# A hybrid DeltaNet and ConvGLU layer on one core: order of the last loads of the scan, place of one weight split, and 64 waits ahead of TensorE's program

## The chip, the cores and the metric

One core of a Trainium2 chip runs the whole layer in one launch. The metric is the device time of the launch in microseconds.

## What is computed

One layer (DEPTH = 1) of a trunk, for 1024 latent tokens (rows of 64) and 128 context tokens that share the weights:

```python
def mixer(h, row_len, s0_f, s0_b, w_in, conv_a_w, qkv_conv_w, a_log, dt_bias, o_norm_w, w_out):
    z = h @ w_in
    ...
    y_conv = cb * row_conv3(cc * cx, conv_a_w, row_len)
    qkv = jax.nn.silu(row_conv3(qkv, qkv_conv_w, row_len)).astype(jnp.float32)
    ...
    o_f, s_f = chunked_gated_delta(q, k, v, beta[:, :, 0], log_alpha[:, :, 0], s0_f)
    ...
    o = rmsnorm(o, o_norm_w) * jax.nn.silu(gate.astype(jnp.float32).reshape(b, l, DN_HEADS, DV))
    y = jnp.concatenate([y_conv, o.reshape(b, l, V_W).astype(h.dtype)], axis=-1) @ w_out
    return y, s_f, s_b

def conv_glu(h, row_len, w_up, ffn_conv_w, w_down):
    u, gt = jnp.split(h @ w_up, 2, axis=-1)
    gt = grid_conv3x3(gt, ffn_conv_w, row_len)
    return (jax.nn.gelu(gt) * u) @ w_down
```

The width is 1024, there are 4 heads of 128, the FFN width is 2816. Around the mixer and the ConvGLU stand RMS norms with shift, scale and gate from `silu(c) @ w_ada + b_ada`. The delta rule runs forward and backward in chunks of 64. Outputs are the two streams after a last norm and the scan's final states of the context tokens.

## The kernel before, in words

Everything is kept with channels on partitions and the 1152 tokens on the free axis, in 3 thirds of 384 or in 9 tiles of 128 (`TT_` = 9, `LAST` = 8, `HALF` = 4, `EARLY` = 6). Each product is made in three passes of fp32r matmuls, with the weights and the activations split in a high and a low part. A *unit* is a 128 x 1024 piece of weights: SP loads it into `raw`, ACT copies the high part (`high`, L1478 to L1481), POOL subtracts to get the low part (`low`, L1280 to L1283), and TensorE waits for the latter (`wl_ready`) and multiplies in `product_step` (L2360 to L2370; L2368 is the matmul with the high activations, L2370 the one with the low ones). Units 0 to 28 are the input projection, `U_OUT` = 29 to 36 the output projection, the rest the FFN. Ahead of all this TensorE makes the modulation rows (`ada_unit`, L2302 to L2309): the weights for them come through a ring of four buffers, whose next load waits until a unit is used.

The order of the work is written out by hand for each engine. Between the input and the output projection lies the scan, with a function for each engine: `delta_pe` (L1147), `delta_act` (L838), `delta_dve` (L925), `delta_pool` (L696), and the loop at L613 on SP. Each runs over x = -1 to 8; with y = x + 1, a round does the serial step x for both directions d = 0, 1 and prepares what step y needs. Direction 0 takes tile y, direction 1 tile 7 - y, and both take tile 8 (the context) last. The steps that matter here, with `seen(eng, what, d, n)` as the wait for the n-th of a kind:

- SP, for each y: the decay rows of both directions into `gb` (L618, waits for `q_decayed` of the round before), `LZ` (L623), keys and values `kv` (L629), queries `q` (L636; direction 0 also waits for `trq`, the turned queries of the round before). At y = 1 the first two gate tiles `og` follow (`og_load`, L608 to L611). At y = 7 and y = 8 half each of the convolution output `ycA` follows (L645, 1152 KB each). Behind the loop come the gate tiles of index 1, 2, 3 and the last, then `ycB`, three units and `X` for the residual.
- POOL: the mask on the decay rows (`masked`, L688), later scale and square of finished tiles (L707, L702), and the decayed queries (`decayed`, L694, waits for `gb_exp` of ACT). At x = 2 the low half of unit 30 (`U_OUT + 1`) stands at the end of the round.
- ACT: exponentials of the masked rows (`exps`, L816), the new values (L874), off-diagonal blocks (L748, L752), `gb_exps` (L824), key scaling (`key_end`, L863), copies (L870, L844), squares of the turned queries (L834), the corner copy (L761), then logarithm and root for the norm (L850, L855). At x = 1 the high half of unit 30 stands behind the key scaling.
- DVE: from x = 6 on, `finish` (L968) multiplies a turned tile with the gate tile `og`; further `diagonal` (L987), `low_diagonal` (L998), `values` (L1007), `weights` (L1021), `second_out` (L953), sums of squares (L960, L962) and the state (L942, L945).
- TensorE: matmuls of the scan (`by_head`, L1157), transposes (`turn`, L1152), the 32-wide products (L1102, L1116, L1118), third and fourth products (L1130, L1142, L1144). `queries` at y = 8 waits for `o_final`, which `finish` gives.

Behind the scan come the output projection (the first pair begins with k = 0 on `ycA` and waits for the state), the second norm, and the FFN in a hardware loop of five turns on each engine (`pe.Fori(0, GROUPS)`, L2618): on TensorE 8 blocks of 72 matmuls and 8 of 36 in each turn, which does 4 of the FFN's 22 column blocks.

```python
            def og_load(d, t, i):
                if i and i < 3:
                    seen(sp, "o_final", d, i)
                sp.dma_start(gate_tile(d, i)[:], g_d[:, :, t * P:t * P + P]).then_inc(s[gate_landed(d, i)], 16)
```

## Time and profile before

| | us |
|---|---|
| median of 3 runs | 1610.46 (1606.65 to 1616.3) |
| the profiled execution | 1610.77 |
| its span, first to last instruction | 1608.8 |
| TensorE matmuls busy | 1533.7 |
| DVE / ACT / POOL busy | 938.6 / 484.4 / 409.1 |
| granted TensorE clock, mean | 0.981 |

Times in the trace are microseconds from the start of the span. PE is TensorE's matmul side and PEld its weight loads, SPq is the queue side of SyncE (the time in which it issues a DMA), "issue" is time in which an engine waited for nothing that the profile shows. A number in brackets behind a row is the idle time of the engine just before it, with what ended it. The granted clock is 1.00 at 2.4 GHz and 0.50 at 1.2 GHz. By time the span falls into the modulation rows and the first norm (0 to 50), input projection (50 to 483), scan (483 to 624), output projection and second norm (624 to 760), FFN (760 to 1570) and the last products and norm.

### The profile page before, as it was taken

The numbers are of one execution on the slowest core, as the hardware profiler recorded it, in microseconds if no ns is written. First come the engines' busy times: TensorE is split into PE (matmuls) and PEld (weight loads), VectorE is DVE, ScalarE is ACT, GpSimd is POOL, SyncE is SP. The second block draws the span as 40 slices with busy tenths as digits, with TensorE's granted clock in tenths as the row PEclk, the third lists the DMA queues.
The fourth block names the chain that finished last, engine by engine and source line by source line (L and its number), as shares of the span: only waits on it lengthen the run. The fifth ranks groups of instructions, "written<-read, shape, count | busy, mean of one in ns | idle before, by whom it ended". The sixth has DMA issues, their size and how long they took to land.

```text
span 1608.8 us, 24001 instructions
## 1 busy us (share of the span) xinstructions
PE 1533.7 (95%) x9744; PEld 1475.7 (92%) x9744; DVE 938.6 (58%) x1398; ACT 484.4 (30%) x904; POOL 409.1 (25%) x204
## 2 busy tenths in 40 slices
PE   5899999999999988999999999999999999999997
PEld 1798999999989877998999999999999999999996
DVE  2752453669997874337875276536643673467257
ACT  4331254221257674225221212121212210222024
POOL 0011111650223552230232132113221421222220
PEclk9899999999999998999999999999999999999999
DMA  9544224542434556110111111111111111111103
GB/s 350 191 184 153 89 73 132 161 125 72 140 118 132 158 185 261 40 66 1 53 40 40 51 37 45 40 41 40 40 40 41 40 53 40 41 40 40 40 1 118
DMA packets 74640, 142.87 MB, mean 89 GB/s; under 512 B 19228, under 2 KB 44900, under 8 KB 72868
## 3 DMA queue, kind: packets, MB, share of 16 engines
q1 hardware_dynamic: 70932, 134.00, 24.7%
q10 hardware_dynamic: 3168, 5.51, 0.9%
q8 instruction: 86, 1.41, 0.4%
q0 software_dynamic: 432, 1.77, 0.3%
q14 instruction: 22, 0.18, 0.0%
HBM read 120.60 MB, written 20.65 MB: 88 GB/s over the span
## 4 chain that ended last, share of the span: by engine, by line
PE 81%; DVE 8%; DMA 4%; ACT 3%; issue 2%; POOL 1%; SPq 1%; DVEq 0%; ACTq 0%; POOLq 0%
PE ps L2368 49%; PE ps L2370 24%; DMA araw<-wts 2%; PE ps L1157 2%; PE ps L2309 1%; DVE ptmp L1978 1%; DVE lanes L1982 1%; PE ps L2319 1%; DMA og<-gd 1%; PE ps L2576 1%; DVE fa L2203 1%; POOL qd L694 1%; PE ps L2477 0%; PE ps L2436 0%; DMA q<-q_d 0%
## 5 line engine op out<-in xcount | busy, mean ns | idle before, releaser
L2368 PE MATMUL ps<-hH,wH 128*128 128x384 f32 x1680 | 570.0, 339 | 8.0 <-DVE hL L1807 3.6
L2370 PE MATMUL ps<-hL,wH 128*128 128x384 f32 x1680 | 565.8, 337 | 7.2 <-issue 7.2
L1283 POOL TENSOR_TENSOR wL<-raw,wH 128x1024 fp32r<-128x1024 f32 x93 | 225.9, 2429 | 906.5 <-ACT wH L1481 906.0
L2368 PE MATMUL ps<-hH,wL 128*128 128x384 f32 x1680 | 384.4, 336 | 0.0
L2368 PEld LDWEIGHTS ps<-hH,wH 128*128 128x128 f32 x1680 | 318.4, 190 | 15.8 <-issue 13.3
L1481 ACT ACTIVATE wH<-raw 128x1024 fp32r<-128x1024 f32 x99 | 105.1, 1061 | 739.8 <-PE ps L2368 738.7
L2370 PEld LDWEIGHTS ps<-hL,wH 128*128 128x128 f32 x1680 | 318.6, 190 | 8.5 <-issue 8.5
L2203 DVE SCALAR_TENSOR_TENSOR fa<-G,cst,fa 128x1024 f32<-128x1024 f32 x176 | 302.2, 1717 | 15.4 <-DVE fa L2200 0.6
L2368 PEld LDWEIGHTS ps<-hH,wL 128*128 128x128 f32 x1680 | 302.1, 189 | 0.0
L2368 PE MATMUL ps<-pH,wH 128*128 128x384 f32 x528 | 179.2, 339 | 4.1 <-DVE pL L2227 1.9
L2090 DVE SCALAR_TENSOR_TENSOR X<-ps,mod,X 128x384 f32<-128x384 f32 x138 | 70.5, 567 | 187.2 <-PE ps L2368 187.2
L2370 PE MATMUL ps<-pL,wH 128*128 128x384 f32 x528 | 177.1, 335 | 0.0
L2368 PE MATMUL ps<-pH,wL 128*128 128x384 f32 x528 | 123.0, 335 | 0.0
L2199 DVE TENSOR_SCALAR fa<-G,cst 128x1024 f32<-128x1024 f32 x22 | 16.6, 753 | 172.2 <-ACT G L1497 172.2
L2368 PEld LDWEIGHTS ps<-pH,wH 128*128 128x128 f32 x528 | 99.6, 189 | 7.0 <-DVE X L2092 3.2
L2370 PEld LDWEIGHTS ps<-pL,wH 128*128 128x128 f32 x528 | 99.5, 189 | 0.7
L2368 PEld LDWEIGHTS ps<-pH,wL 128*128 128x128 f32 x528 | 94.8, 189 | 0.0
L1839 DVE TENSOR_SCALAR acc<-zp,wqk 128x1024 f32<-128x1024 f32 (+1 forms) x24 | 21.8, 946 | 72.8 <-ACT zp L1497 72.8
L1342 POOL TENSOR_TENSOR pL<-fa,pH 128x1152 fp32r<-128x1152 f32 x16 | 58.9, 3680 | 12.3 <-ACT pH L1701 12.3
L2309 PE MATMUL ps<-araw,scT 128*32 128x512 f32 x192 | 37.3, 675 | 18.2 <-DMA araw<-wts 18.2
L2220 DVE TENSOR_TENSOR fa<-fa,ps 128x384 f32<-128x384 f32 x66 | 32.6, 550 | 20.0 <-PE ps L2368 20.0
L2309 PEld LDWEIGHTS ps<-araw,scT 128*32 128x32 f32 x192 | 5.9, 114 | 41.3 <-DMA araw<-wts 29.1
(326 smaller groups left out, 1872.7 us busy)
## 6 DMA issues: line engine op xcount, KB each, us to landing
raw<-wts SPq DMA_DIRECT2D x103, 512.0 KB, 3.3
araw<-wts SPq DMA_DIRECT2D x48, 512.0 KB, 6.2
X<-xT SPq DMA_DIRECT2D x8, 1152.0 KB, 14.5
kv<-tok_d SPq DMA_DIRECT2D x16, 512.0 KB, 5.1
tok_d<-stage ACTq DMA_DIRECT2D x18, 256.0 KB, 2.1
q<-q_d SPq DMA_DIRECT2D x18, 256.0 KB, 6.8
gb<-grow_d SPq DMA_DIRECT2D x18, 256.0 KB, 3.8
y<-X SPq DMA_DIRECT2D x8, 384.0 KB, 2.4
```

What stands on the lines that cost most here:

```text
L1157: last = M(ps[:, k, h * P:h * P + P], left(h), right(h), start=(start if start is not None else h == 0), stop=(stop if stop is not None el ...
L1283: nc.gpsimd.tensor_tensor(weight(1, u4), raw[:, u4 % RAW, :], weight(0, u4).bitcast(F32), ALU.subtract).then_inc(s["wl_ready"], 1)
L1342: nc.gpsimd.tensor_tensor(pL[:, slot, :], fa[:, f % 2, :], pH[:, slot, :].bitcast(F32), ALU.subtract).then_inc(s["pL_ready"], 1)
L1481: A(weight(0, u4), raw[:, u4 % RAW, :], ACT.Copy).then_inc(s["wh_ready"], 1)
L1839: last = V.tensor_scalar(dst, src, w(tap), None, ALU.mult)
L2090: last = V.scalar_tensor_tensor(xs(lo, hi), bank3(side, n)[:, 0:hi - lo], mod[:, gate * 8 + ob, 0:1], xs(lo, hi), ALU.mult, ALU.add)
L2199: V.tensor_scalar(dst, src, w(3 * dy + dx), None, ALU.mult)
L2203: last = V.scalar_tensor_tensor(dst, src, w(3 * dy + dx), dst, ALU.mult, ALU.add)
L2220: last = V.tensor_tensor(fa[:, f4 % 2, n * TW:n * TW + TW], fa[:, f4 % 2, n * TW:n * TW + TW], bank3(side, n), ALU.mult)
L2309: last = M(ps[o:o + Q, ada_bank(m), :], scT[:, kt, :], araw[:, a % ARAW, 512 * j:512 * j + 512], start=(kt < 2), stop=(kt >= KT - 2))
L2368: last = M(out, lhs, rh[:, c], start=(k == 0 and not lo), stop=(lo and k == kts - 1))
L2370: M(out, lhs, rl[:, c], start=False, stop=False)
```

## The change

- On SP, y = 8 begins with the two gate tiles of index 1, which stood behind the loop, and the query load of direction 0. The query load of direction 1 for y = 8 is left out (its only readers are at y < 8).
- The two loads of `ycA` go from SP to ACT, at the beginning of its rounds x = 5 and x = 7, with the same waits.
- On POOL, the low half of unit 30 goes from the end of round x = 2 to right behind the masks of that round. On ACT, its high half goes from behind the key scaling of round x = 1 to behind the corner copy.
- TensorE's program begins with 128 waits for `bias_set`, which DVE sets with its third instruction; two waits go into one instruction, so that there are 64 instructions more.

```diff
+N_PAD = 128
@@ SP
+            def q_load(d, y):
+
+                t = tile_of(d, y)
+                seen(sp, "qk", d, min(y, HALF))
+                seen(sp, "q_decayed", d, y)
+                if d == 0:
+                    sp.wait_ge(s["trq"], y)
+                sp.dma_start(dl[d]["q"][:], q_d[:, :, t * P:t * P + P]).then_inc(s[f"q_in_{d}"], 16)
+
             for y in range(1, TT_):
+                if y == LAST:
+                    for d in range(2):
+                        og_load(d, tile_of(d, 5), 1)
+                    q_load(0, y)
                 for d in range(2):
...
-                for d in range(2):
-                    b, t = dl[d], tile_of(d, y)
-                    seen(sp, "qk", d, min(y, HALF))
-                    seen(sp, "q_decayed", d, y)
-                    if d == 0:
-                        sp.wait_ge(s["trq"], y)
-                    sp.dma_start(b["q"][:], q_d[:, :, t * P:t * P + P]).then_inc(s[f"q_in_{d}"], 16)
+                if y < LAST:
+                    for d in range(2):
+                        q_load(d, y)
...
-                if y in (HALF + 3, HALF + 4):
-                    k = y - HALF - 3
-                    seen(sp, "pt", 1, (HALF + 2, LAST)[k])
-                    sp.dma_start(ycA[:, 2 * k:2 * k + 2, :].bitcast(F32), yc_d[:, 4 * k:4 * k + 2, :].bitcast(F32)).then_inc(s["ycA_in"], 16)
-            for d in range(2):
-                og_load(d, tile_of(d, 5), 1)
@@ POOL
+                if x == 2:
+                    low(U_OUT + 1, U_OUT + 1)
                 for d, t, i in summed(x - 1):
                     scale(d, t, i)
...
-                if x == 2:
-                    low(U_OUT + 1, U_OUT + 1)
@@ ACT
+                if x in (HALF + 1, LAST - 1):
+                    k = (HALF + 1, LAST - 1).index(x)
+                    seen(act, "pt", 1, (HALF + 2, LAST)[k])
+                    act.dma_start(ycA[:, 2 * k:2 * k + 2, :].bitcast(F32),
+                                  yc_d[:, 4 * k:4 * k + 2, :].bitcast(F32)).then_inc(s["ycA_in"], 16)
                 if 0 < y < TT_:
                     exps(y)
...
-                    if y == 2:
-                        high(U_OUT + 1, U_OUT + 1, 0)
...
                     corner(y)
+                if y == 2:
+                    high(U_OUT + 1, U_OUT + 1, 0)
@@ TensorE
+            for _ in range(N_PAD):
+                pe.wait_ge(s["bias_set"], 1)
             pe.wait_ge(s["sc_ready"], 2)
             for a in range(KT + 1):
                 ada_unit(a)
```

## Rows read from the trace of the kernel before

**Rows 1.** The page, busy time by engine.
```profile
PE 1533.7 (95%) x9744; PEld 1475.7 (92%) x9744; DVE 938.6 (58%) x1398; ACT 484.4 (30%) x904; POOL 409.1 (25%) x204
```
**Rows 2.** Waits of TensorE, 480 to 625: us in total, times, longest.
```profile
PE ps L2368 <- DVE S L942: 7.0, 1, 7.0
PE ps L1157 <- DVE oTok L968: 6.6, 1, 6.6
PE ps L1157 <- ACT Y L874: 3.4, 2, 2.8
```
**Rows 3.** Chain of waits, 583 to 604: start us, us, what.
```profile
584.53 2.95 POOL qd L694
...
591.77 0.61 SPq L645
...
592.43 9.72 DMA og<-gd
```
**Rows 4.** Timeline of DVE, ACT and TensorE, 579 to 611: start us, us, instructions.
```profile
579.79 1.41 DVE L968 SCALAR_TENSOR_TENSOR oTok<-ps,onw,og 128x512 f32<-128x512 f32 x2
...
591.81 2.44 ACT L816 ACTIVATE R<-R,SC 128x128 f32<-128x128 f32 x8
...
596.68 0.27 ACT L752 ACTIVATE TX<-ps 32x128 f32<-32x128 f32 x1
...
602.24 1.57 DVE L968 SCALAR_TENSOR_TENSOR oTok<-ps,onw,og 128x512 f32<-128x512 f32 x2 [6.92 <-DMA og<-gd]
...
608.99 1.06 PE L1152 MATMUL ps<-cst,q 128*128 128x128 f32 x4
...
610.08 0.28 ACT L834 ACTIVATE ptmp<-ps 128x128 f32<-128x128 f32 x1 [10.67 <-PE ps L1152]
```
**Rows 5.** Windows: busy time of each engine, granted clock, DMA share, GB/s.
```profile
603.00:606.00 3.00, 2.75 (x15) 2.56 (x16) 1.95 (x3) 0.00 (x0) 0.00 (x0) 0.50 0.45 122
```
**Rows 6.** Timeline of ACT, TensorE, POOL and DVE around unit 30, 504 to 524.
```profile
504.02 1.04 ACT L1481 ACTIVATE wH<-raw 128x1024 fp32r<-128x1024 f32 x1
...
505.83 0.63 PE L1152 MATMUL ps<-cst,q 128*128 128x128 f32 x4 [0.66 <-ACT KQ L870]
...
520.94 2.36 POOL L1283 TENSOR_TENSOR wL<-raw,wH 128x1024 fp32r<-128x1024 f32 x1
...
521.42 2.74 DVE L987 TENSOR_TENSOR raw<-XT,cst 128x512 f32<-128x512 f32 x1
```
**Rows 7.** Waits of TensorE in the FFN loop, 760 to 1400.
```profile
PE ps L2370 <- issue: 7.2, 4, 2.2
PE ps L2368 <- issue: 2.5, 4, 0.9
```
**Rows 8.** Timeline of TensorE at the second turn of the FFN loop.
```profile
1073.16 0.43 PE L2368 MATMUL ps<-hH,wH 128*128 128x384 f32 x1 [0.91 <-issue]
...
1076.24 0.69 PE L2370 MATMUL ps<-hL,wH 128*128 128x384 f32 x1 [1.94 <-issue]
```
**Rows 9.** Windows of 6 us behind the first three turns.
```profile
921.00:927.00 6.00, 6.00 (x26) 6.00 (x27) 2.73 (x4) 2.78 (x6) 1.56 (x1) 0.72 0.28 90
1076.00:1082.00 6.00, 5.75 (x18) 5.76 (x19) 3.13 (x4) 2.38 (x6) 1.15 (x1) 0.50 0.25 90
1232.00:1238.00 6.00, 5.52 (x24) 5.52 (x25) 2.76 (x4) 2.76 (x6) 1.52 (x1) 0.72 0.27 90
```
**Rows 10.** DMA view 1070 to 1078 (queue: packets, MB, share); windows between instruction packets.
```profile
q8 instruction: 3, 0.05, 2.2%
...
1007.00:1029.00 22.00, 21.68 (x125) 21.36 (x125) 13.90 (x19) 3.29 (x3) 4.80 (x2) 1.00 0.15 49
1051.40:1070.60 19.20, 19.20 (x113) 19.20 (x112) 3.59 (x8) 1.06 (x1) 2.38 (x1) 1.00 0.18 55
```
**Rows 11.** TensorE's first matmul, and a wait by itself in SP's chain of waits.
```profile
5.42 1.92 PE L2309 MATMUL ps<-araw,scT 128*32 128x512 f32 x4 [5.42 <-DMA araw<-wts]
...
589.32 0.02 SPq L386
589.34 0.03 issue
```

## The prediction

> **What bounds the kernel now.** I read the views in this order: the page, the waits of TensorE by stage, the chain of waits, the timeline of the delta stage, the granted clock by window, and the DMA view of the instruction queue. The page says that TensorE is busy for 95% of the span [rows 1], so a gain has to come from one of its few idle stretches or from a stretch at the lower clock. The waits of the delta stage (480 to 625) name two of about 7 us: one before L2368, which is the end of the scan, and one before L1157, put down to DVE's L968 [rows 2]. The chain shows what L968 itself waited for: POOL's second product of round y = 7 ends at 587.49, SP then works through its list for y = 8, reaches the convolution load at 591.77 and the gate loads at 592.43, and the gate tile lands 9.72 us later, at 602.15 [rows 3]. Round y = 8 therefore stands still: DVE is idle for 6.92 us, from 595.3 to 602.24 [rows 4]. The wait before L2368 is a chain of small steps on ACT, POOL and DVE and is not touched. The third place is the FFN loop: at each of its four turns TensorE stops twice with no releaser, 2.5 us in all for the first stops and 7.2 us for the second ones [rows 7].
>
> **The gate loads, the query load and the convolution output on ACT's queue.** SP now issues the two gate loads as the first thing of y = 8. They need the first two tiles finished (L968, at 579.8 to 581.2 [rows 4]), so they go out at about 581.5, while SP has nothing to send until 584.6, and land by about 591 even if they take the 9.72 us of the old ones. Nothing is queued behind them that was ready earlier. Next, the query load of direction 0 waits for the turned queries of y = 7, which PE finishes about 585.4; the decay row of direction 0 behind it then leaves at about 586.1 instead of 584.6, and its mask at 589.4. That is not late, for ACT starts the exponentials only at 591.81 [rows 4]. The decay row of direction 1 waits for the POOL product that ends at 587.49 as before. The query load of direction 1 is dropped; nobody waits for it.
> The convolution load moves to ACT, ahead of the exponentials of y = 6 and y = 8. At y = 6 ACT waits for a mask there anyway, so I cost it at nothing; without that cover it costs the 0.61 us that SP needs for it [rows 3]. At y = 8 it is on the path: 0.61 us. What comes out: DVE runs L968 at 595.35 and 596.1 instead of 602.24; off-diagonal blocks on ACT end at 597.6 instead of 596.95 [rows 4], and now the third products wait for them. Then come third products (0.6 at the full clock), the copy (0.4), second third products and copy (to 599.5), two weights of 0.65 (to 600.8), and the turned queries at 600.8 instead of 608.99 [rows 4]: 8.2 us earlier. The part after the old wait ran at the lower clock, 0.50 [rows 5], which the shorter idle time avoids, and this is why the shift exceeds the wait. From L834 (610.08) on, everything is the old chain, shifted. I take **7.5 us**, bounds 6.0 (the wait less the ACT issue) and 8.5. What is late next is the off-diagonal block on ACT.
>
> **Unit 30.** ACT's high half (0.95 to 1.04 us) stands today between the key scaling and the copy for which TensorE waits 0.66 us at 505.83 [rows 6]. Moved behind the corner copy it falls into 1.5 us in which ACT waits for PE: gain **0.7 us**, bounds 0 and 1.0. POOL's low half (2.36 us at 520.94) moves some 11 us ahead, into idle time before the products of y = 3, which wait for ACT until 518.2: cost nothing; if that cover were gone, 2.4 us. Today it lies beside DVE's L987, which takes 2.74 us instead of about 1.05 [rows 6]. By the Trainium skill (SBUF — State Buffer, on the shared port pair) a GpSimd instruction and a DVE instruction with two SBUF inputs shut each other out; the row agrees. But TensorE has no gap there, and ACT takes up the result only 0.3 us after it was free, so I book no gain for it. A stall of 2.8 us at 548.6 [rows 2] starts with the POOL products of y = 4 that take 5.95 us beside DVE's work. A shift of under 1 us may or may not dissolve it; I leave it, and keep 2.8 us for the range.
>
> **64 instructions at TensorE's head.** 128 waits for a semaphore set at 0.9, two in one instruction. TensorE starts at 5.42, released by a DMA [rows 11], so 4.4 us of cover. A wait that stands by itself on SP takes 0.05 us (0.02 and an issue of 0.03) [rows 11]: 64 of them 3.2 us. Cost nothing; uncovered, all of what exceeds 4.4 us, since the loads behind the first unit wait for it.
> What they do is move the rest of TensorE's program by 64 places. The instruction queue brings 0.05 MB in 3 packets, 16 to 17 KB each, around the turn at 1073 [rows 10]. In steady running a packet comes each 22 us, in which the window counts 125 matmuls and as many weight loads [rows 10], so a packet holds about 250 instructions. At the turn one packet goes out at 1070.6, TensorE restarts at 1073.16, runs 5 matmuls and stops 1.94 us [rows 8]; the next packet is at 1074.0 and it runs on 2.2 us later. So the border between two packets lies 5 matmuls behind the head of the loop, and the second one is asked for only when the first is entered. With 64 instructions in front, that border moves 32 matmuls back, ahead of the loop's head, and the next is about 95 matmuls (16 us) behind the head, which hides a fetch of 2.2 us. The four second stops go: **7.2 us** [rows 7]. With them goes the slow clock behind them: 6 us at 0.72, 0.50 and 0.72 after the first three turns are 1.7, 3.0 and 1.7, together **6.4 us** [rows 9]; the fourth had 1.00.
> What may come back is at the first stop. Before the turn the last border is 19.2 us (113 matmuls) back [rows 10]; the 64 instructions add 32 matmuls to that, which is more than one packet holds, so one more border comes to stand 7 to 15 matmuls (1.2 to 2.6 us) before the turn. A fetch takes 2.2 to 2.6 us from packet to use, so the fetch for what follows the loop may be under way when the turn asks for its own. Bounds 0 and 1.4 us each turn; no row shows two fetches at once, I take the middle, **2.8 us** back for four. Net 10.8, bounds 13.6 and (if the gap stays and takes the clock with it) about 0.
>
> **The sum.** The profiled execution took 1610.77 us (span 1608.8, 2.0 around it), 0.3 above the median of 1610.46. 1610.8 - 7.5 - 0.7 - 10.8 = 1591.8, taken as 1592.
>
> **The rivals.** *A: the loop gives nothing.* The second stop belongs to the turn and not to the border, or the first one grows by as much. For it: I know the borders only from packet times. Against it: the stop came after exactly 5 matmuls each time, and the packet stands in it. 1610.8 - 8.2 = 1602.6. The Trainium skill (Runtime: NRT & Kernel Launch, "Instruction fetch mechanics") has fetches in blocks of 256 instructions, calls a crossing mostly hidden and makes only the taken branch outside the window dear; by its words alone this rival holds, while the size of block agrees with the packets. Chance 0.18.
> *B: another load takes the place of the gate tile.* Keys and values for y = 8 leave SP at 590 and the convolution output still goes at 591.8, onto the same 16 engines; if values landed at 600, the tail would give 3 and the total 1596. Against it: two query tiles and two gate tiles less are on the engines then. Chance 0.12.
> *C: slower.* The waits at the head are dear. They decide from 0.07 us each on, and make the whole slower than before from (19.0 + 4.4) / 64 = 0.37 us each. At the 0.61 us of an instruction that SP issues [rows 3] they take 39 us, 34.6 beyond the cover: 1592 + 34.6 = 1627. Against it: the 0.05 us of SP's wait. Chance 0.03.
> *D: the stall of y = 4 goes too*, 1589. Chance 0.10. The forecast has 0.57.
>
> **How the numbers follow.** The forecast's own bounds are 1610.8 - 8.5 - 0.7 - 13.6 = 1588 and 1610.8 - 6.0 - 8.0 = 1597. B lies inside; D at the good end reaches 1585, and A lies at 1602.6 (at worst 6.0 alone, 1604.8), so the range goes from 1585 to 1603.5; C is left out. A measurement of this kernel can tell 0.5%, 8 us, from no change. Forecast, B and D are faster than 1602.4; A lies on that bound and is split, a third of it faster. Faster 0.85, same 0.12, slower 0.03.
>
> **What would show it.** Right: no wait of DVE L968 for the gate load of 7 us; L1152 near 600; a single stop per turn in the loop, under 2 us, followed by a clock of 1.00; first matmul still at 5.4; the two POOL masks of y = 4 no later than 523.3. Wrong: two stops per turn, or one of 3 us with the clock at 0.5 behind it; L1157 before the last round waiting for ACT or a DMA for over 3 us; the first matmul after 6 us.

## The result, and the profile after

| | before | changed |
|---|---|---|
| median, us | 1610.75 (1606.65 to 1616.3, 4 runs) | 1593.2 (1591.28 to 1595.0, 4 runs) |
| ratio | | 0.9889, interval 0.9856 to 0.9921 |
| profiled execution, us | 1610.77 | 1592.61 |
| span, us | 1608.8 | 1590.7 |
| TensorE matmuls busy, us | 1533.7 | 1524.4 |
| granted clock, mean | 0.981 | 0.985 |

The change makes the kernel 17.5 us faster, 1.1%; the forecast was 1592.0. That the sum is right does not say that its terms are: the loop gave more than its term and the scan less, as the section on the prediction shows. The page, busy time by engine, against [rows 1]:

```profile
PE 1524.4 (96%) x9744; PEld 1471.3 (92%) x9744; DVE 936.8 (59%) x1398; ACT 484.4 (30%) x904; POOL 403.1 (25%) x204
```

The same number of matmuls takes 9.3 us less, so about half of the gain is work done at a higher clock, the rest idle time that has gone.

**By stage.** Each cut is an instruction that is easy to find in the timelines: the first matmul of the first norm's output (hH), ACT's first exponentials (those of y = 1), its exponentials of y = 7 and of y = 8, the first matmul on `ycA`, and the first matmul on `pH`, the input of the FFN's second product. The last cut lies some 90 us behind the start of the loop, within its first turn, so the first FFN products belong to the row of the output projection. Below, "FFN" is the stretch from that cut to the end; all four returns to the head of the loop lie in it. The first stretch counts from the start of the span.

| us | before | changed | difference |
|---|---|---|---|
| start to the first matmul on hH | 50.6 | 47.2 | -3.4 |
| to the exponentials of y = 1 | 426.8 | 427.6 | +0.8 |
| rounds: exponentials of y = 1 to y = 7 | 98.8* | 100.2 | +1.4 |
| last stretch: y = 7 to the first matmul on ycA | 48.0 | 42.5 | -5.5 |
| output projection, second norm, first FFN products | 230.2 | 232.9 | +2.7 |
| rest of the FFN and the end | 754.3 | 740.3 | -14.0 |

(* the six rounds took 15.0, 16.8, 16.0, 16.5, 15.8 and 18.7 before; 16.1, 16.9, 15.0, 16.5, 16.8 and 18.9 after.)

**The FFN loop.** Waits of TensorE, 760 to 1400, in the changed kernel (engine, line, waited for: us in total, times, longest). Against [rows 7] the line of the second stops, 7.2 us in four, is gone; the first ones, 2.5 us before, are as they were:

```profile
PE ps L2379 <- issue: 2.3, 4, 0.8
```

The timeline of TensorE at the first turn, changed kernel (start us, us, instructions, idle before). One stop, and then it runs on; before, there was a second one after the fifth matmul [rows 8]:

```profile
913.99 0.43 PE L2379 MATMUL ps<-hH,wH 128*128 128x384 f32 x1 [0.44 <-issue]
914.26 0.34 PE L2381 MATMUL ps<-hL,wH 128*128 128x384 f32 x1
914.44 0.35 PE L2379 MATMUL ps<-hH,wH 128*128 128x384 f32 x1
914.62 0.34 PE L2381 MATMUL ps<-hL,wH 128*128 128x384 f32 x1
914.80 0.34 PE L2379 MATMUL ps<-hH,wH 128*128 128x384 f32 x1
914.98 0.33 PE L2381 MATMUL ps<-hL,wH 128*128 128x384 f32 x1
```

The windows of 6 us behind the first three turns, changed kernel (us, busy time and count of PE, PEld, DVE, ACT and POOL, granted clock, DMA share, GB/s). They had a clock of 0.72, 0.50 and 0.72 with 26, 18 and 24 matmuls [rows 9]:

```profile
914.80:920.80 6.00, 6.00 (x36) 6.00 (x36) 0.93 (x2) 4.86 (x8) 2.40 (x1) 1.00 0.18 61
1066.00:1072.00 6.00, 6.00 (x37) 6.00 (x36) 0.95 (x2) 4.75 (x8) 2.40 (x1) 1.00 0.21 57
1217.00:1223.00 6.00, 6.00 (x36) 6.00 (x36) 0.94 (x2) 4.86 (x8) 2.39 (x1) 1.00 0.20 61
```

**The end of the scan.** Timeline of SP, POOL, ACT, DVE and TensorE, 579 to 602, changed kernel. The gate tiles go out at 579.11 and DVE's `finish` (now L977) waits for the turned tile, 0.31 us, and no longer for the load, 6.92 us [rows 4]. The turned queries come at 601.02 and ACT's squares at 601.72, against 608.99 and 610.08 [rows 4]:

```profile
579.11 1.76 SPq L612 DMA_DIRECT2D og<-gd  x2
...
589.33 1.27 POOL L692 TENSOR_TENSOR R<-gb,cst 128x512 f32<-128x512 f32 x1 [5.48 <-DMA gb<-grow_d]
...
590.97 1.28 ACT L859 ACT_TABLE_LOAD   x1
...
590.99 0.33 ACTq L885 DMA_DIRECT2D ycA<-yc  x1
...
595.66 1.41 DVE L977 SCALAR_TENSOR_TENSOR oTok<-ps,onw,og 128x512 f32<-128x512 f32 x2 [0.31 <-PE ps L1161]
...
601.02 0.66 PE L1161 MATMUL ps<-cst,q 128*128 128x128 f32 x4 [0.62 <-DVE PT L1030]
...
601.72 0.28 ACT L838 ACTIVATE ptmp<-ps 128x128 f32<-128x128 f32 x1 [1.81 <-PE ps L1161]
```

Waits of TensorE, 480 to 625, changed kernel. Of the three in [rows 2] the middle one is gone; the one at the end of the scan and the one of y = 4 (2.8 us, for the new values of ACT) stand:

```profile
PE ps L2379 <- DVE S L951: 7.0, 1, 7.0
PE ps L1166 <- ACT Y L878: 2.9, 2, 2.8
```

**The head.** Waits of TensorE, 0 to 60, changed kernel, and its first matmul, which stood at 5.42 [rows 11]. It now starts at 8.01, released by nothing that the profile shows: TensorE's sequencer was still going through the 64 instructions. The third view below lists 63 instructions that do nothing but wait (the last of the 128 waits share instructions with what follows): 51 ns each, the first starting at 1.0 and the last at 7.7, so one in 0.11 us.

```profile
PE ps L2318 <- DMA araw<-wts: 11.0, 6, 5.2
PE ps L2318 <- issue: 8.0, 1, 8.0
```

```profile
8.01 1.93 PE L2318 MATMUL ps<-araw,scT 128*32 128x512 f32 x8 [8.01 <-issue]
```

```profile
L2333 PEldq EVENT_SEMAPHORE  x63: 51/51/51, 1.0 to 7.7; - x63
```

### The profile page after: what moved, and what is told of

It is laid out like the page before. It is cut to its first block, busy times and chain, and to the rows that moved or that the text cites. A ratio compares the mean times of both kernels' runs of the same rounds, so it can differ in the third digit from the quotient of the medians.

```text
span 1590.7 us, 24063 instructions
## 1 busy us (share of the span) xinstructions
PE 1524.4 (96%) x9744; PEld 1471.3 (92%) x9744; DVE 936.8 (59%) x1398; ACT 484.4 (30%) x904; POOL 403.1 (25%) x204
## 4 chain that ended last, share of the span: by engine, by line
PE 85%; DVE 7%; ACT 2%; issue 2%; DMA 2%; POOL 1%; DVEq 0%; ACTq 0%; SPq 0%; POOLq 0%
PE ps L2379 50%; PE ps L2381 25%; PE ps L1166 4%; DMA araw<-wts 2%; PE ps L2318 1%; DVE ptmp L1987 1%; DVE lanes L1991 1%; PE ps L2328 1%; POOL qd L698 1%; PE ps L2587 1%; DVE fa L2212 1%; DMA gb<-grow_d 1%; PE ps L2488 1%; PE ps L2447 0%; DVE XT L1998 0%
## 5 line engine op out<-in xcount | busy, mean ns | idle before, releaser
L2212 DVE SCALAR_TENSOR_TENSOR fa<-G,cst,fa 128x1024 f32<-128x1024 f32 x176 | 295.9, 1681 | 15.4 <-DVE fa L2209 0.6
L1351 POOL TENSOR_TENSOR pL<-fa,pH 128x1152 fp32r<-128x1152 f32 x16 | 55.5, 3471 | 21.1 <-ACT pH L1710 21.1
L2318 PE MATMUL ps<-araw,scT 128*32 128x512 f32 x192 | 33.5, 664 | 19.1 <-DMA araw<-wts 11.0
```

Of the source, the lines that this page charges most:

```text
L1351: nc.gpsimd.tensor_tensor(pL[:, slot, :], fa[:, f % 2, :], pH[:, slot, :].bitcast(F32), ALU.subtract).then_inc(s["pL_ready"], 1)
L2212: last = V.scalar_tensor_tensor(dst, src, w(3 * dy + dx), dst, ALU.mult, ALU.add)
L2318: last = M(ps[o:o + Q, ada_bank(m), :], scT[:, kt, :], araw[:, a % ARAW, 512 * j:512 * j + 512], start=(kt < 2), stop=(kt >= KT - 2))
```

## The experiments

Twelve kernels in three sets. The kernel before ran beside each set: 1610.05 (1601.82 to 1617.7, 29 runs) for the first four, 1608.63 (1603.27 to 1610.42, 11) for the next four, 1611.27 (1601.7 to 1617.23, 11) for the last. One kernel's executions spread by up to 0.6% to either side, so a difference of 2 or 3 us between two medians tells little alone; below, the stages of the profiles are read beside it. The three sets ran on different chips. A comparison across sets is safer by what each kernel gains on the kernel before of its own set, and where the text gives such a gain it is the difference of the two medians. The ratios in the table differ slightly from the ratios of these medians; by its ratio the kernel with the waits alone gains 9.7 us and not 11.3.

| kernel | median us (lowest to highest, runs) | ratio to before, interval |
|---|---|---|
| waits only | 1598.8 (1592.58 to 1608.49, 12) | 0.994, 0.9917 to 0.9963 |
| all but the waits | 1604.72 (1597.34 to 1608.14, 12) | 0.9967, 0.9946 to 0.9989 |
| waits later | 1593.25 (1591.8 to 1594.7, 4) | 0.9897, 0.9857 to 0.9937 |
| 4 instructions, not 64 | 1609.0 (1600.2 to 1611.66, 10) | 0.9985, 0.9962 to 1.0009 |
| gate and query loads early | 1587.21 (1586.02 to 1590.46, 4) | 0.987, 0.9849 to 0.989 |
| unit 30 moved | 1596.46 (1594.09 to 1599.09, 6) | 0.9928, 0.991 to 0.9946 |
| convolution output on ACT | 1600.52 (1593.84 to 1606.86, 6) | 0.9943, 0.9922 to 0.9964 |
| decay rows before the query | 1593.06 (1590.76 to 1599.12, 6) | 0.9916, 0.9896 to 0.9937 |
| convolution output back on SP | 1590.39 (1585.78 to 1598.31, 6) | 0.9871, 0.9839 to 0.9903 |
| only its second half on ACT | 1594.58 (1590.33 to 1598.13, 6) | 0.9893, 0.9864 to 0.9923 |
| last diagonal block later | 1589.34 (1587.4 to 1591.96, 6) | 0.9863, 0.9835 to 0.9891 |
| the change once more | 1593.11 (1589.74 to 1595.76, 6) | 0.9883, 0.9854 to 0.9912 |

The stages of their profiles in us, cut as above. "3-4" is from the exponentials of y = 3 to those of y = 4; "last" is y = 7 to the first matmul on `ycA`, with the part behind the exponentials of y = 8 in brackets.

| kernel | start to hH | to y = 1 | 3-4 | last (behind y = 8) | output, to pH | FFN, from pH |
|---|---|---|---|---|---|---|
| before | 50.6 | 426.8 | 16.0 | 48.0 (32.5) | 230.2 | 754.3 |
| changed | 47.2 | 427.6 | 15.0 | 42.5 (25.0) | 232.9 | 740.3 |
| waits only | 53.5 | 428.2 | 16.0 | 43.7 (25.9) | 230.0 | 740.6 |
| all but the waits | 52.9 | 427.0 | 15.0 | 40.1 (24.0) | 232.9 | 750.4 |
| waits later | 52.9 | 426.3 | 15.0 | 41.8 (23.5) | 230.4 | 740.7 |
| 4 instructions | 48.1 | 427.7 | 15.0 | 41.0 (23.9) | 230.4 | 758.8 |
| gate and query early | 48.7 | 426.8 | 16.0 | 39.3 (24.0) | 232.7 | 740.2 |
| unit 30 moved | 51.7 | 426.6 | 15.0 | 49.0 (33.4) | 230.0 | 740.9 |
| conv. on ACT | 53.3 | 428.1 | 16.0 | 48.4 (32.7) | 232.9 | 740.5 |
| rows before query | 49.6 | 427.6 | 15.0 | 42.5 (27.2) | 232.8 | 740.4 |
| conv. back on SP | 52.5 | 428.4 | 15.0 | 40.1 (25.0) | 234.1 | 741.2 |
| second half on ACT | 49.4 | 426.3 | 15.0 | 41.9 (26.8) | 230.0 | 740.6 |
| diagonal later | 48.6 | 428.9 | 15.0 | 41.6 (26.0) | 229.9 | 740.6 |
| change once more | 49.1 | 428.4 | 15.0 | 40.1 (25.0) | 232.7 | 740.0 |

### First set: the waits

**The waits alone**, in the kernel before.

```diff
+N_PAD = 128
...
+            for _ in range(N_PAD):
+                pe.wait_ge(s["bias_set"], 1)
             pe.wait_ge(s["sc_ready"], 2)
```

> The kernel before with the 128 waits alone. Border theory (the waits move the border between two instruction packets away from the loop's head): in the FFN loop one stop per turn instead of two, no slow clock behind the turns, and from the first product with pH to the end 14 us less than before; the scan as before. Head theory (the later start of the modulation rows, 8.0 instead of 5.4 us, lets the loads of X through): the first product with hH at about 47 instead of 50.6. Both together 1595; if the waits only move the border and the head is chance, 1597. Rival (the loop's gain needs the other edits): 1608 or more.

Measured: 1598.8, that is 11.3 us below 1610.05. The FFN takes 740.6 instead of 754.3. The first matmul on hH was expected at about 47 by the theory that the later start lets other loads through; it came at 53.5, so that theory is out. Waits of TensorE in the loop: one kind of stop is left.

```profile
PE ps L2371 <- issue: 2.7, 4, 0.9
```

**Everything but the waits.**

```diff
-            for _ in range(N_PAD):
-                pe.wait_ge(s["bias_set"], 1)
             pe.wait_ge(s["sc_ready"], 2)
```

> The changed kernel without the waits at the head. Border theory: two stops per turn as before, 2.5 and 7.2 us; the scan shorter by some 2 to 7 us. If the recorded sum were right (the tail of the scan gives 7.5 and unit 30 gives 0.7) the time is 1602.5; if the profile of the changed kernel is typical (the scan took 1.9 us less in it, and 2.7 were lost behind it) it is 1607 to 1609.

Measured: 1604.72, 5.3 us below the kernel before. Both stops of the loop are there, the second one again behind five matmuls, in the waits and in the timeline of TensorE:

```profile
PE ps L2379 <- issue: 7.5, 4, 2.1
PE ps L2377 <- issue: 2.4, 4, 0.7
```

```profile
913.81 0.44 PE L2377 MATMUL ps<-hH,wH 128*128 128x384 f32 x1 [0.69 <-issue]
...
916.87 0.69 PE L2379 MATMUL ps<-hL,wH 128*128 128x384 f32 x1 [1.92 <-issue]
```

So the two halves of the change each work without the other, and the whole of the loop's gain hangs on the 64 instructions. The FFN takes 750.4 us here and 754.3 before, with the same stops (9.9 and 9.7 us in all): what differs is the clock behind them, as the kernel with 4 instructions shows below. In this profile the round from y = 5 to y = 6 took 13.9 us instead of 15.5 to 17.6 elsewhere, and the next one 20.4 instead of 18.0 to 18.9: what one round wins there, the next gives back.

**The waits later**: not at the start of TensorE's program but behind the second turn of the modulation rows, so that the first matmul is not held up and the rest of the program is moved by the same 64 places.

```diff
-            for _ in range(N_PAD):
-                pe.wait_ge(s["bias_set"], 1)
             pe.wait_ge(s["sc_ready"], 2)
             for a in range(KT + 1):
                 ada_unit(a)
...
+            for _ in range(N_PAD):
+                pe.wait_ge(s["bias_set"], 1)
```

> The changed kernel with the same 128 waits moved from the head to behind the second turn of the modulation rows, where TensorE is idle for 3.6 us before the first product with hH. Border theory: the loop as in the changed kernel, one stop per turn, 2.3 us in four. Head theory: the first matmul at 5.4 again, the modulation rows as before; 64 instructions of 0.11 us are 7 us, 3.5 of them uncovered, so the first product with hH at 52 to 54 and the time 1597 to 1600.

Measured: 1593.25, the time of the change. The first matmul starts at 5.32 again, but nothing is gained by it: TensorE's waits from 0 to 60 are 17.8 us for the loads where the changed kernel has 8.0 and 11.0, and the kernel before 18.0 us of the same kind. The waits of this kernel, and of the kernel before:

```profile
PE ps L2318 <- DMA araw<-wts: 17.8, 8, 5.3
```

```profile
PE ps L2309 <- DMA araw<-wts: 18.0, 9, 5.4
```

TensorE stands still for 17.8 to 18.2 us in the four kernels without waits at the head (the 4 instructions counted among them), and for 19.0 to 20.6 us in the ten with them, 8.0 of it at the head: the weights come through a ring of four buffers, and most of a late start is time that it would wait for them later. In the new place, the expectation had 3.5 us of the 64 instructions uncovered. Only 0.3 are: TensorE is idle for 3.9 us ahead of hH and not for 3.6, because the sequencer began on them while the matmuls before them, which run from 45.45 to 48.99, were still under way:

```profile
L2347 PEldq EVENT_SEMAPHORE  x62: 51/51/51, 45.7 to 52.3; - x62
```

The start to hH lies between 47.2 and 53.5 us in these profiles with the waits in front and without them, so it is the loads of one execution that set it. The 3.4 us of the changed kernel's profile there are no part of the change.

**Four instructions in place of 64.** This keeps waits at the head and takes away what they do to the borders of the instruction fetch.

```diff
-N_PAD = 128
+N_PAD = 8
```

> The changed kernel with 8 waits, which make 4 instructions, instead of 128. Border theory: the border comes to stand 4 instructions nearer to the loop's head, so that the second stop of each turn comes after 3 matmuls instead of 5, and is longer by the 0.35 us of two matmuls; time as without the waits or up to 2 us more. Rival (the second stop belongs to the turn and not to the border): still after 5 matmuls.

Measured: 1609.0, no gain that can be told against 1610.05, although the scan's part of the change is in it, and 4.3 us above the kernel without waits, where at most 2 were expected. The waits in the loop and the timeline of TensorE at the first turn:

```profile
PE ps L2381 <- issue: 9.6, 4, 2.6
...
PE ps L2379 <- issue: 1.8, 4, 0.5
```

```profile
911.55 0.44 PE L2379 MATMUL ps<-hH,wH 128*128 128x384 f32 x1 [0.41 <-issue]
911.83 0.34 PE L2381 MATMUL ps<-hL,wH 128*128 128x384 f32 x1
912.01 0.34 PE L2379 MATMUL ps<-hH,wH 128*128 128x384 f32 x1
914.81 0.44 PE L2381 MATMUL ps<-hL,wH 128*128 128x384 f32 x1 [2.47 <-issue]
```

The stop now comes behind three matmuls instead of five. A matmul has its weight load beside it, so two matmuls are four instructions, and four instructions is what was added. The stop is at a fixed place in the program, and moves through it one for one. It is also longer, 9.6 against 7.2 us for four; two matmuls less to run before the border (0.36 us, for four turns 1.4) are part of that. The FFN takes 758.8 us, 4.5 more than before: 2.4 more in the second stops and 0.7 less in the first ones make 1.7 of it, and the rest is work at the lower clock.

That part changes from profile to profile. The 20 us behind the second return to the head, in the kernel before, in the one with everything but the waits, and here:

```profile
1073.00:1093.00 20.00, 17.91 (x86) 17.59 (x87) 10.12 (x13) 7.12 (x10) 3.44 (x2) 0.83 0.08 28
```

```profile
1069.00:1089.00 20.00, 18.06 (x103) 17.74 (x104) 12.85 (x14) 7.51 (x10) 6.32 (x3) 1.00 0.10 33
```

```profile
1067.00:1087.00 20.00, 17.47 (x85) 17.15 (x86) 9.88 (x13) 7.14 (x10) 3.20 (x2) 0.83 0.09 28
```

Over the four returns the granted clock of such windows is 0.91, 0.83, 0.91 and 1.00 before, 0.91, 1.00, 1.00 and 1.00 without the waits, and 0.91, 0.83, 0.83 and 0.91 here, so that of the 80 us in these windows 7.0, 1.8 and 10.4 are lost against full speed. The second stop is there in every turn; the slow clock behind it follows in some turns and not in others, and what decides it is not shown. With the 64 instructions the clock is 1.00 behind every return.

### Second set: the parts in the scan, each on top of the waits alone

**The gate and query loads early**, with the convolution output left on SP.

```diff
+                if y == LAST:
+                    for d in range(2):
+                        og_load(d, tile_of(d, 5), 1)
+                    q_load(0, y)
                 for d in range(2):
...
...
+                if y < LAST:
+                    for d in range(2):
+                        q_load(d, y)
...
-            for d in range(2):
-                og_load(d, tile_of(d, 5), 1)
```

(`q_load` is the one of the change, in place of the loop over the query loads.)

> The kernel before with the 128 waits and, of the scan's edits, only the gate and query loads ahead of y = 8 (the convolution output stays on SP). Theory of the record (the late gate tile costs the last round 6 to 8 us): from the exponentials of y = 8 to the first product with ycA 23.5 to 25 us instead of 32.5, and 4 to 7 us less than with the waits alone: 1592 to 1595. Rival (the gate tile was late only in the profiled execution of before; with the waits alone that stretch took 25.9): 1 to 2 us less than with the waits alone, 1597.

Measured: 1587.21, the lowest median of all kernels here, 11.6 us below the waits alone, or 10.2 when each is taken against the kernel before of its own set. The intervals, 0.9849 to 0.989 and 0.9917 to 0.9963, lie apart. The last stretch takes 39.3 us. Waits of TensorE, 590 to 640, with none for the gate tile among them:

```profile
PE ps L2378 <- DVE S L950: 7.0, 1, 7.0
```

**Unit 30 moved.**

```diff
@@ POOL
+                if x == 2:
+                    low(U_OUT + 1, U_OUT + 1)
                 for d, t, i in summed(x - 1):
                     scale(d, t, i)
...
-                if x == 2:
-                    low(U_OUT + 1, U_OUT + 1)
@@ ACT
...
-                    if y == 2:
-                        high(U_OUT + 1, U_OUT + 1, 0)
...
+                if y == 2:
+                    high(U_OUT + 1, U_OUT + 1, 0)
```

> The kernel before with the 128 waits and only unit 30's two halves moved. From the exponentials of y = 3 to those of y = 4 15.0 us instead of 16.0, the round before unchanged at 16.9; DVE's L987 beside the former place of the low half takes 1.05 instead of 2.7 us. The time 1 us less than with the waits alone, 1598; if the moved high half also shortened its round, 1597.

Measured: 1596.46, 2.3 us below the waits alone, or 0.9 when each is taken against the kernel before of its own set; the intervals overlap, so only the profiles can tell. The table seems to say where: round 3-4 takes 15.0 us in every kernel that has this edit and 16.0 in every one that has not, and its neighbour 2-3, in which the high half stood, takes 16.9 with it and 16.8 without. That points to the low half, and it is wrong, for the edit moves the cut itself: the high half now stands right ahead of the exponentials of y = 3 and holds them up, which makes round 2-3 look as long as before and 3-4 shorter.

The order of TensorE's and DVE's instructions is the same in both kernels, so the same instruction can be followed. From the L934 with which DVE begins its new values at 491.65 in the kernel before, to the same one of the next round, at 508.48, the four kernels without the edit take 16.83 us and the ten with it 15.97, 0.86 less. From there to the L945 at 532.27, past the place where the low half stood, all take 23.8. The next 8.6 us, up to the L979 at 540.86, are 0.2 shorter in eight of the ten, and why is not shown. The 0.86 come out where the high half stood. The same stretch of TensorE before and with the edit:

```profile
504.01 1.16 PE L1157 MATMUL ps<-Y,PTb 128*128 128x128 f32 x8
505.83 0.63 PE L1152 MATMUL ps<-cst,q 128*128 128x128 f32 x4 [0.66 <-ACT KQ L870]
...
507.28 1.16 PE L1157 MATMUL ps<-S,QKV 128*128 128x128 f32 x8
```

```profile
505.18 1.16 PE L1158 MATMUL ps<-Y,PTb 128*128 128x128 f32 x8
506.18 0.60 PE L1153 MATMUL ps<-cst,q 128*128 128x128 f32 x4
...
507.60 1.16 PE L1158 MATMUL ps<-S,QKV 128*128 128x128 f32 x8
```

The wait of 0.66 us is gone, and 3.27 us have become 2.42. ACT and DVE with the edit: the high half ahead of the exponentials of y = 3, and DVE's L988 in 1.04 us where it took 2.74 beside POOL's subtraction [rows 6]:

```profile
509.59 1.06 ACT L1482 ACTIVATE wH<-raw 128x1024 fp32r<-128x1024 f32 x1
510.55 2.43 ACT L817 ACTIVATE R<-R,SC 128x128 f32<-128x128 f32 x8
...
521.74 1.04 DVE L988 TENSOR_TENSOR raw<-XT,cst 128x512 f32<-128x512 f32 x1
```

So the low half did leave DVE's way, but TensorE gains nothing by it there.

The wait for the gate tile is as it was: TensorE waits 5.8 us for DVE's `finish` (L969).

**The convolution output on ACT.**

```diff
@@ SP
-                if y in (HALF + 3, HALF + 4):
-                    k = y - HALF - 3
-                    seen(sp, "pt", 1, (HALF + 2, LAST)[k])
-                    sp.dma_start(ycA[:, 2 * k:2 * k + 2, :].bitcast(F32), yc_d[:, 4 * k:4 * k + 2, :].bitcast(F32)).then_inc(s["ycA_in"], 16)
@@ ACT
+                if x in (HALF + 1, LAST - 1):
+                    k = (HALF + 1, LAST - 1).index(x)
+                    seen(act, "pt", 1, (HALF + 2, LAST)[k])
+                    act.dma_start(ycA[:, 2 * k:2 * k + 2, :].bitcast(F32),
+                                  yc_d[:, 4 * k:4 * k + 2, :].bitcast(F32)).then_inc(s["ycA_in"], 16)
```

> The kernel before with the 128 waits and only the convolution output on ACT's queue. The gate tile leaves SP 0.6 us earlier but lands with the same bytes around it. From the exponentials of y = 6 to those of y = 8 up to 0.6 us more, the rest as before: 1598 to 1600. If the convolution load ahead of the gate tile is what makes it late, the last round falls to 24 to 25 us and the time to 1594.

Measured: 1600.52, against 1598.8 for the waits alone: no gain. Against the kernel before of its own set it is 3.1 us worse than the waits alone, with intervals that overlap. With the big load off SP's list, the gate tiles still come late, and TensorE waits 5.2 us for what needs them:

```profile
PE ps L1159 <- DVE oTok L970: 5.2, 1, 5.2
```

ACT issues the load in 0.33 us (SP needed 0.61 in the kernel before [rows 3]).

**The decay rows before the query load**, in the changed kernel: SP's y = 8 then has the gate tiles first and the rest in its old order.

```diff
                 if y == LAST:
                     for d in range(2):
                         og_load(d, tile_of(d, 5), 1)
-                    q_load(0, y)
...
-                if y < LAST:
-                    for d in range(2):
-                        q_load(d, y)
+                for d in range(2 if y < LAST else 1):
+                    q_load(d, y)
```

> The changed kernel with SP's query load of y = 8 back behind the decay rows, LZ, keys and values (the gate tiles stay first). In the changed kernel POOL waits 5.5 us for the decay row of y = 8, and the exponentials of y = 6 to y = 8 are 36.4 us apart instead of 34.2. If the wait for the turned queries ahead of the decay rows is the cause, that stretch falls to about 34.5 and the time to 1591.5; if the collisions of DVE and POOL are the cause, no difference, 1593.

Measured: 1593.06, in a set in which the changed kernel did not run; the ratio, 0.9916, is a little worse than the 0.9883 and 0.9889 of the change, with intervals that overlap. The masks of y = 8 come earlier (586.62 and 589.56, not 589.33 and 590.96), and y = 7 to y = 8 takes 15.3 us instead of the 17.5 of the changed kernel's profile. But this is not due to the order: the change once more, with the queries first, took 15.1. And with the rows first TensorE waits for the queries:

```profile
PE ps L1164 <- DMA q<-q_d: 2.7, 1, 2.7
```

and the part behind y = 8 takes 27.2 instead of 25.0. The whole last stretch is 42.5 with this order, and 42.5 and 40.1 in the two profiles of the change. Nothing speaks for the rows first.

### Third set: what the convolution load costs, and the stall of y = 4

**The changed kernel with both halves of the convolution output back on SP.** The diff is the one above, the other way round, in the changed kernel.

> The changed kernel with both halves of the convolution output back on SP, behind the query loads of y = 7 and the keys and values of y = 8. Additive theory (the gate and query loads gave 11.6 of 1598.8 with the waits, unit 30 gives 1.0 more, and the move to ACT costs the rounds y = 6 to y = 8 some 3 us): 1586, the rounds y = 5 to 6 and y = 7 to 8 at 15.8 and 15.3 us as in the run with the gate and query loads alone. Rival (that run was merely lucky in its collisions): 1592 to 1593 like the changed kernel.

Measured: 1590.39, against 1593.11 for the changed kernel in the same set, between the two forecasts and with intervals that overlap. The round y = 5 to 6 took 16.8 us, as in the changed kernel, and y = 7 to 8 took 15.1, as in the change once more. The place of the load sets neither.

**With only the second half on ACT.**

```diff
@@ SP
+                if y == HALF + 3:
+                    k = 0
+                    seen(sp, "pt", 1, (HALF + 2, LAST)[k])
+                    sp.dma_start(ycA[:, 2 * k:2 * k + 2, :].bitcast(F32), yc_d[:, 4 * k:4 * k + 2, :].bitcast(F32)).then_inc(s["ycA_in"], 16)
@@ ACT
-                if x in (HALF + 1, LAST - 1):
-                    k = (HALF + 1, LAST - 1).index(x)
+                if x == LAST - 1:
+                    k = 1
```

> The changed kernel with the first half of the convolution output back on SP and the second still on ACT. If the first half costs (it leaves 20 us earlier on ACT and shares the engines with keys, values and queries of y = 6), the time is that of both halves on SP, 1586; if the second half costs (0.6 us of ACT ahead of the exponentials of y = 8, and its bytes), it is 1589 to 1593, with 24.6 us or more from those exponentials to the first product with ycA.

Measured: 1594.58. The three medians, 1590.39 with none on ACT, 1594.58 with the second half and 1593.11 with both, point to a cost of the second half of some 3 us, but their intervals overlap. On ACT itself it costs nothing that the timeline shows: the issue at 590.99 lies beside the table load of 590.97 to 592.25 in the changed kernel. I leave open what the 3 us are, and whether there are any.

**The last diagonal block later**, on top of the convolution output back on SP. TensorE's stall of y = 4 begins with POOL's two products of that round, which take 6.33 us beside DVE's `diagonal(LAST)`. It is moved two rounds on, behind the low diagonal blocks of x = 5.

```diff
+                if x == 5:
+                    dve.wait_ge(s["wl_ready"], U_OUT + 2)
+                    dve.wait_ge(s["solved"], 3)
+                    diagonal(LAST)
...
-                if 0 < x < 4:
+                if 0 < x < 3:
...
-                    if x == 3:
-                        dve.wait_ge(s["wl_ready"], U_OUT + 2)
-                        dve.wait_ge(s["solved"], 3)
```

> Both halves of the convolution output on SP, and DVE's two L987 for y = 8 moved from the end of round x = 3, where they hold up POOL's second product of y = 4, to behind the low diagonal of round x = 5, where DVE waits 2.5 us for TensorE. Theory: POOL's pair takes 3 instead of 6 us, the second decay row of y = 5 leaves 3 us earlier, the wait of 2.8 us for new values at y = 5 goes: 2 to 3 us less than with both halves on SP, 1583. Rival: DVE's L1022 alone (two SBUF inputs, 1.3 us) holds POOL up as long as before: no difference.

Measured: 1589.34, against 1590.39: no difference that can be told. The mechanism did part of what was expected: POOL's pair of products takes 4.43 us, where 3 were expected, and the wait goes. POOL's pair of y = 4, without the edit and with it:

```profile
537.82 6.33 POOL L702 TENSOR_TENSOR qd<-gb,q 128x512 f32<-128x512 f32 x2 [7.92 <-ACT gb L832]
```

```profile
534.67 4.43 POOL L702 TENSOR_TENSOR qd<-gb,q 128x512 f32<-128x512 f32 x2 [8.20 <-ACT gb L832]
```

The round from y = 4 to y = 5 takes 15.1 us instead of 16.5, and TensorE's wait for the new values is 0.3 us instead of 2.8.

The last stretch is 1.5 us longer in return (41.6 against 40.1), so the 1.4 us saved are not seen at the end of the scan.

**The changed kernel once more**, beside the three above.

> The changed kernel itself, beside the three above on the same chip: 1593, the rounds y = 5 to 6 at 15.7 to 17, y = 7 to 8 at 16 to 18, and about 24 us behind them.

Measured: 1593.11 (0.9883, interval 0.9854 to 0.9912), against 1593.2 in the first measurement. Its last stretch took 40.1 us, 2.4 less than in the profile shown first, while its output projection took 232.7 again.

## Why the prediction was right

**The bound.** Right: TensorE is at 96% after as at 95% before, and the gain came out of the two places named, the wait of y = 8 and the turns of the loop.

**The sum.** 1592.0 against 1593.2, and in part by luck. The mechanisms of the loop, the gate loads and the high half are the ones that the runs show, but the loop's term was too small (10.8; 11.3 by the medians, 14.0 in the profiles) and the scan's too big (8.2; 5.3 by the medians of the kernel without the waits), and the two errors pull against each other.

**The loop: the step that had the wrong size.** The forecast was 7.2 us of stops and 6.4 us of clock, 13.6, less 2.8 given back at the first stops. The FFN got 14.0 us shorter, and by the medians the waits bring 11.3 alone (9.7 by the ratio) and 11.5 on top of the rest (1604.72 against 1593.25 for the waits later). The 7.2 of stops come back in every profile with the old borders; the 6.4 of clock are those of one execution, in which they were 7.0 over the longer windows, while another had 1.8. So the median has less of them than the profile of the kernel before.

The border theory is shown, by four kinds of evidence: the stop moves by two matmuls for four instructions, it is gone with 64, it does not matter where in front the 64 stand (740.7 with the waits later), and all eleven profiles with 64 instructions have an FFN of 740.0 to 741.2, the three others 750.4 to 758.8.

The term that was mis-sized is "2.8 us back for four" at the first stops. A further instruction packet does go out ahead of the turn's own (at 908.6, then 911.4 and 914.4 in the changed kernel), as worked out, but the first stops are 2.0 to 3.3 us in four in the eleven profiles, 2.6 in the mean, against 2.5 and 2.4 in the kernel before and the one without the waits. I took the middle of two bounds, 0 and 5.6, where the lower one was near the truth. Why nothing came back stays open: the two packets lie 2.8 us apart, about as long as a fetch takes, so it is not shown that two fetches were ever under way at once.

Rival A is out: by it the FFN would not have changed. The Trainium skill (Runtime: NRT & Kernel Launch, "Instruction fetch mechanics"), on which that rival could lean, calls a crossing from one block of instructions to the next mostly hidden. In steady running the traces agree: there are 86 packets in the span, and the waits of TensorE list no stop without a releaser but those of the loop. Three or five matmuls behind a taken branch they do not: there a crossing cost 1.8 to 2.4 us in the mean of four turns (7.2, 7.5 and 9.6 us in all), and here the measurement decides.

**The waits at the head: costed at nothing, and nothing was lost, but not for the reason given.** I took 0.05 us each from a wait on SP, 3.2 us in all under a cover of 4.4. They took (8.01 - 0.9) / 64 = 0.11 us each, 7.1 in all, and held TensorE up by 2.6 us. This is above the 0.07 from which rival C was to begin. What saved the time is a cover that I had not seen: TensorE stands 18.0 us waiting for the same loads in the rows that follow, so most of what it starts late is time that it would have waited. With the waits later the time is the same, 1593.25. The step "uncovered, all of what exceeds 4.4 us" was wrong, and the sign "the first matmul after 6 us" showed the mis-sized wait and not a loss.

**The gate loads: right in mechanism, too big in the mean.** The turned queries were to come 8.2 us earlier, at 600.8; they came at 601.02, 8.0 earlier, and the squares 8.4. Behind the exponentials of y = 8 the old order takes 32.5 to 33.4 us (before, unit 30 moved, convolution output on ACT), the new one 23.5 to 27.2 in ten profiles. The whole last stretch, which counts what lies between y = 7 and y = 8 as well, is 48.0 to 49.0 against 39.3 to 42.5; the profile first shown, with 5.5 us gained against the 7.5 forecast, is at the poor end of that. One profile does not fit: with the waits alone the stretch was 43.7, since the exponentials of y = 8 came 2.3 us later and the gate tile was then only 1.8 us late. The medians of the parts add as well as can be told, if each kernel is taken against the kernel before of its own set: on top of the 11.3 us of the waits alone, the loads give 10.2, unit 30 0.9 and the convolution output on ACT -3.1, together 8.0, and the change has 6.3 and 6.9 more than the waits in its two measurements. The change without its waits gives 5.3 us by the medians, forecast 8.2 for the scan.

"That is not late", said in the prediction of the masks of y = 8 behind the query load, was nearly so. They came at 589.33 as forecast (589.4), the second one at 590.96, and in the change once more the exponentials wait 0.26 and 0.45 us for them. Taken back, the order gains nothing. Rival B did not come: nothing took the gate tile's place at 595.66 but the off-diagonal block on ACT (596.45), which I had named.

**The convolution output: right in the sum, wrong in the row.** I costed the issue at 0.61 us from SP's row; on ACT it is 0.33, and at y = 8 it lies beside a table load. That should make this part free, yet the kernel without it is 2.7 us lower by the medians of the same set, within the intervals. Nothing shows a gain from it.

**Unit 30: right, in size and in half.** Forecast 0.7 us from the high half and nothing from the low one; measured 0.86 where the high half stood, nothing where the low one stood, and 0.2 behind them that is not explained. That TensorE has no gap beside DVE's slow L987, as I had read, was the right reason to book nothing for the low half. The Trainium skill (SBUF — State Buffer, the shared port pair) says that a GpSimd instruction and a DVE instruction with two SBUF inputs shut each other out. The rows agree: L987 takes 2.74 us beside POOL's subtraction [rows 6], and the same instruction without it 1.04.

**Rival D**, that the stall of y = 4 goes too: not in the changed kernel (2.8 us stand). Moving the diagonal block dissolves it, and brings nothing that can be measured.

**What the forecast did not have**: the output projection. Up to the first matmul on `pH` it takes 229.9 to 230.4 us in some profiles and 232.7 to 234.1 in others, and the profile of the change has one of the latter. The difference is clock, in two places. The first is behind the wait at the end of the scan, which is 7.0 us in both: the 10 us behind it. The second is behind a stop of 2.0 us some 32 us later, for POOL's low half of a unit: the 10 us from 30 us on. In the changed kernel, and in the kernel before:

```profile
617.50:627.50 10.00, 9.98 (x44) 9.90 (x45) 2.17 (x4) 2.63 (x5) 3.03 (x3) 0.69 0.99 408
647.50:657.50 10.00, 7.97 (x38) 7.65 (x37) 5.44 (x9) 3.59 (x4) 4.74 (x2) 0.83 0.31 105
```

```profile
624.30:634.30 10.00, 10.00 (x54) 9.94 (x55) 2.60 (x5) 3.33 (x6) 3.36 (x4) 0.82 1.01 399
654.30:664.30 10.00, 8.23 (x47) 8.23 (x48) 4.30 (x6) 3.17 (x3) 4.11 (x2) 1.00 0.32 105
```

The first place costs 1.1 us by the time at which the 54th matmul starts, the second 1.5 more. Seven of the fourteen profiles have the one kind and seven the other; those with 0.69 to 0.74 in the first window all have 0.83 in the second, and those with 0.79 to 0.85 all have 1.00. (The 234.1 have a third slow stretch, some 155 us behind the first matmul on `ycA`.) The slower one comes with the convolution output on ACT (232.9) and with it on SP (gate and query loads early, 232.7), and without the waits (232.9); the changed kernel with the waits later has the faster one (230.4). So it is no part of the change that can be named, and what decides it stays open.

**A smaller change that does as much.** The kernel before with the 64 instructions and the gate and query loads early, its convolution output left on SP and unit 30 where it was, has 1587.21 us, a ratio of 0.987; with unit 30 moved as well it is 1590.39, 0.9871. Both ratios are a little under the 0.9883 and 0.9889 of the change, by 2 to 3 us, with intervals that overlap. So they are no worse than the change, and that they are better is not shown.

## What to carry to other kernels

When an engine stops with no releaser a few instructions behind the head of a loop, shift its program by a few instructions and look whether the stop moves with it; if it does, enough filler ahead of the loop takes it away, and with it the slow clock that may follow it. A load that someone waits for at the end of a stage belongs in the queue where its own condition is met, not where the list of the round happens to reach it; ask first what else stands in that queue, since here the load that was moved off another engine's queue gave nothing. A late start costs nothing where the engine waits for the same loads anyway, so cover is to be looked for behind a delay as well as beside it. And before a gain is put down to one stage of a table, make sure that the edit has not moved the instruction at which the stages are cut; an engine whose program the edit leaves alone is the better ruler.

## What the runs showed of the hardware

- A satisfied wait is not free on TensorE: 64 instructions with two waits each took 7.1 us, 0.11 each, twice what a wait by itself takes on SP (0.05, [rows 11]). Where they stood behind matmuls still under way, the sequencer went through them beside these, and only 0.3 us of the 7 were left over (the waits later).
- A border of the instruction fetch costs 1.8 to 2.4 us in the mean where it lies five or three matmuls behind the taken branch of a loop (kernel before, 4 instructions), and nothing that can be seen once the program is moved by 64 instructions. One more packet some 3 us ahead of the branch's own left the branch's stop nearly as it was (2.6 us in four turns in the mean of eleven profiles, against 2.4 and 2.5).
- The clock behind the same two stops of a turn is not fixed: the 20 us behind the second return had a granted clock of 0.83 in two profiles and 1.00 in a third.
- Issuing the same 1152 KB load took 0.33 to 0.35 us on ACT's queue in every profile, and on SP's 0.61 in most and 0.42 to 0.94 in others; on ACT it went beside a table load.
- A wait of the same length, 7.0 us at the end of the scan, was followed by a granted clock of 0.82 over the next 10 us in one profile and 0.69 in another, and the clock behind a stop of 2.0 us 32 us later differed with it, 1.00 and 0.83.
